# Sliding-window attention: both parts of the keys in one score matmul, summed on VectorE

## The reference

```python
s = jnp.einsum('bcqhgd,bckhd->bchgqk', qc, kb) * (D ** -0.5)
sink = sinks.reshape(1, 1, Hkv, G, 1, 1)
m = jnp.maximum(jnp.max(s, axis=-1, keepdims=True), sink)
e = jnp.exp(s - m)
p = e / (jnp.sum(e, axis=-1, keepdims=True) + jnp.exp(sink - m))
out = jnp.einsum('bchgqk,bckhd->bcqhgd', p, vb)
...
x = x + rmsnorm(out @ w_out, g[1])
h = rmsnorm(x, g[2])
```

## Time and profile before

| what | before |
|---|---|
| runs | 2272.24, 2273.50, 2275.01 us |
| profiled execution: span on the core | 2273.9 us |
| mean granted TensorE clock | 0.993 of full |
| PE busy | 2234.7 us (98%), 11331 matmuls |
| DVE, ACT, POOL busy | 1756.8 (77%), 1183.6 (52%), 840.9 us (37%) |
| steps of the sliding attention (first `turn` to last) | 1452.5 to 1603.4 us |

### The profile page before, as it was taken

How to read it: one execution, slowest core, us unless ns; L and a number is a source line. 1 busy time by engine, 2 the same in 40 slices (tenths; PEclk the granted TensorE clock), 3 DMA queues, 4 the chain that set the end, 5 groups by cost and what they waited for, 6 DMA issues and landing times. The chain is left out here.

```text
span 2273.9 us, 31830 instructions
## 1 busy us (share of the span) xinstructions
PE 2234.7 (98%) x11331; PEld 1890.4 (83%) x11331; DVE 1756.8 (77%) x2694; ACT 1183.6 (52%) x1951; POOL 840.9 (37%) x750
## 2 busy tenths in 40 slices
PE   7999999999999999999999999999999999999998
PEld 6888889999888888888888878888888888888886
DVE  4886789955547888888799867756598888888986
ACT  5658888766433444444444644655444444434453
POOL 3103346310001677777400022222047777771000
PEclk9999999999999999999999999999999999999999
DMA  5111110000422222222663542411322222228435
GB/s 168 36 43 54 29 38 29 11 1 1 167 102 62 77 84 84 84 84 84 217 219 102 185 133 61 107 38 57 108 68 84 84 84 84 84 71 302 150 126 184
DMA packets 190360, 215.18 MB, mean 95 GB/s; under 512 B 15508, under 2 KB 136692, under 8 KB 190204
## 3 DMA queue, kind: packets, MB, share of 16 engines
q1 hardware_dynamic: 185052, 195.81, 27.3%
q10 hardware_dynamic: 5152, 17.34, 2.0%
HBM read 170.77 MB, written 39.98 MB: 93 GB/s over the span
## 5 line engine op out<-in xcount | busy, mean ns | idle before, releaser
L123 PE MATMUL trunk_ps<-l_bhi,l_ahi 128*128 128x512 f32 x528 | 206.0, 390 | 0.5 <-DVE l_blo L3014 0.4
L123 PE MATMUL trunk_ps<-l_bhi,l_alo 128*128 128x512 f32 x528 | 205.5, 389 | 0.0
L123 PE MATMUL trunk_ps<-l_blo,l_ahi 128*128 128x512 f32 x528 | 205.5, 389 | 0.0
L123 PE MATMUL trunk_ps<-l_t_hi,l_s_lo 128*128 128x512 f32 x456 | 177.4, 389 | 0.0
L123 PE MATMUL trunk_ps<-l_t_lo,l_s_hi 128*128 128x512 f32 x456 | 177.4, 389 | 0.0
L123 PE MATMUL trunk_ps<-l_t_hi,l_s_hi 128*128 128x512 f32 x456 | 177.4, 389 | 0.0
L2628 POOL TENSOR_TENSOR l_s_lo<-l_raw,l_s_hi 128x512 fp32r<-128x512 f32 x90 | 157.7, 1760 | 44.9 <-ACT l_s_hi L2539 44.9
L2415 ACT ACTIVATE l_ahi<-l_a 128x512 fp32r<-128x512 f32 x132 | 83.3, 631 | 158.5 <-PE trunk_ps L123 141.5
L2628 POOL TENSOR_TENSOR l_s_lo<-l_w_sum,l_s_hi 128x512 fp32r<-128x512 f32 x76 | 120.0, 1580 | 57.1 <-ACT l_s_hi L2539 56.9
L216 POOL TENSOR_TENSOR wring_w_lo<-wring_raw,wring_w_hi 128x256 fp32r<-128x256 f32 x72 | 56.7, 820 | 192.8 <-ACT wring_w_hi L211 192.8
L123 PE MATMUL trunk_ps<-rest_hi,l_s_lo 128*128 128x512 f32 x304 | 118.3, 389 | 0.0
(11 more groups left out here) (485 smaller groups left out, 6732.7 us busy)
## 6 DMA issues: line engine op xcount, KB each, us to landing
l_draw<-in_ffn_w_out SPq DMA_DIRECT2D x154, 256.0 KB, 2.8
l_raw<-in_ffn_w_in SPq DMA_DIRECT2D x48, 512.0 KB, 4.6
gated_dram<-l_gate_out SPq DMA_DIRECT2D x44, 512.0 KB, 2.6
l_a<-gated_dram SPq DMA_DIRECT2D x88, 256.0 KB, 3.9
wring_raw<-in_even_w_in SPq DMA_DIRECT2D x20, 512.0 KB, 3.9
l_raw_g<-in_ffn_w_in SPq DMA_DIRECT2D x20, 512.0 KB, 3.8
l_raw_v<-in_ffn_w_in SPq DMA_DIRECT2D x20, 512.0 KB, 4.9
l_wt<-in_ffn_w_out SPq DMA_DIRECT2D x22, 256.0 KB, 6.4
```

The costliest lines, as they stand in the source:

```text
L123: mm = pe.matmul(o, w, m, start=a, stop=z, skip_group_check=onto)
```

## The change

The two parts of the keys of one head lie side by side (`keys[kv]`, hi then lo), and a pair's scores are one matmul whose moving operand is 2 x 128 columns (2 x 64 for chunk 0): hi products land in one half of a 256-column output, lo products in the other. The scores of all four pairs now fill the whole of `ps[0]`, so steps n and n+1 share one tile and PE waits for `S_summed` of step n-1 pair by pair. ScalarE copies the lo half of two pairs at a time into `s_lo` (`lo_scores`, L1067 of the new kernel). VectorE's `greatest` is, for each pair, one `tensor_tensor_reduce` (L1377): -0.125 times the sum of the hi half in PSUM and `s_lo`, written to `prob[n % 3]`, with the minimum of these and the negated sink as `nbias`. ScalarE's `exp` works in place on `prob` with scale -1. `prob` has three buffers, the third where the last query group lay. ScalarE's order changes: `lo_scores(n+1)`, `copy(n)`, `exp(n+1)`, `sink_exp(n)`; and ahead of slot 0 as in the diff.

```diff
-        self.prob = [at(f"prob{i}", [P, self.PAIRS, P], F32, W + 2 * KB * i) for i in range(2)]
...
-        self.k_hi = [at(f"k_hi{i}", [P, T], F32R, k_at + 4 * KB * i) for i in range(2)]
-        self.k_lo = [at(f"k_lo{i}", [P, T], F32R, k_at + 4 * KB * (2 + i)) for i in range(2)]
+        self.keys = [at(f"k{i}", [P, 2, T], F32R, k_at + 8 * KB * i) for i in range(2)]
+        self.k_hi, self.k_lo = ([k[:, part, :] for k in self.keys] for part in range(2))
...
+        self.prob = [at(f"prob{i}", [P, self.PAIRS, P], F32, a) for i, a in enumerate((W, W + 2 * KB, fm_at + 8 * KB))]
...
+        self.s_lo = at("s_lo", [P, self.PAIRS, P], F32, K + 128 * KB)
...
-        self.S, self.TR = ([ps[i][:, HALF * h:HALF * h + HALF] for h in range(2)] for i in (0, 1))
+        self.S = ps[0].rearrange("p (u part k) -> p u part k", u=self.PAIRS, part=2)
+        self.TR = [ps[1][:, HALF * h:HALF * h + HALF] for h in range(2)]
...
+        def lo_scores(n):
+            nk = self.keys_of(self.where(n)[1])
+            if n:
+                sc.wait_ge(self.S_summed, 4 * n)
+            for h in range(2):
+                sc.wait_ge(self.S_ready, 2 * n + h + 1)
+                pair = slice(2 * h, 2 * h + 2)
+                sc.activation(self.s_lo[:, pair, 0:nk], self.S[:, pair, 1, 0:nk], ACT.Copy).then_inc(self.S_lo, 1)
+
         def exp(n):
             nk = self.keys_of(self.where(n)[1])
-            sc.wait_ge(self.nb_ready, n + 1)
-            if n >= 2:
-                sc.wait_ge(self.T_ready, n - 1)
             for u in range(self.PAIRS):
-                ins = sc.activation(self.prob[n % 2][:, u, 0:nk], self.S[n % 2][:, u * P:u * P + nk], ACT.Exp,
-                                    bias=self.nbias[:, n % self.ROWS, u:u + 1], scale=0.125)
+                if u % 2 == 0:
+                    sc.wait_ge(self.S_summed, 4 * n + u + 2)
+                prob = self.prob[n % 3][:, u, 0:nk]
+                ins = sc.activation(prob, prob, ACT.Exp, bias=self.nbias[:, n % self.ROWS, u:u + 1], scale=-1.0)
             ins.then_inc(self.exp_done, 1)
...
+        lo_scores(0)
+        pack_queries(N_V - 1)
         exp(0)
-        pack_queries(N_V - 1)
+        lo_scores(1)
+        take(N_V)
         exp(1)
-        take(N_V)
+        lo_scores(2)
         for n in range(self.LAST_SLOT):
+            if 2 <= n < NG - 1:
+                lo_scores(n + 1)
+            if n < NG:
+                copy(n)
             if 1 <= n < NG - 1:
                 exp(n + 1)
             if n < NG:
-                copy(n)
                 sink_exp(n)
...
-            if n >= 2:
-                pe.wait_ge(self.exp_done, n - 1)
             for u in range(self.PAIRS):
-                out = self.S[n % 2][:, u * P:u * P + self.keys_of(c)]
-                queries = self.queries_of(self.PAIRS * kv + u, c)
-                pe.matmul(out, queries, self.k_hi[kv][:, self.window(c)], start=True, stop=False)
-                mm = pe.matmul(out, queries, self.k_lo[kv][:, self.window(c)], start=False, stop=True)
-            mm.then_inc(self.S_ready, 1)
+                if n and u % 2 == 0:
+                    pe.wait_ge(self.S_summed, 4 * (n - 1) + u + 2)
+                mm = pe.matmul(self.S[:, u, :, 0:self.keys_of(c)], self.queries_of(self.PAIRS * kv + u, c), self.keys[kv][:, :, self.window(c)],
+                               start=True, stop=True)
+                if u % 2:
+                    mm.then_inc(self.S_ready, 1)
...
-                mm = pe.transpose(self.TR[n % 2][0:nk, u * P:(u + 1) * P], self.prob[n % 2][:, u, 0:nk], ident)
+                mm = pe.transpose(self.TR[n % 2][0:nk, u * P:(u + 1) * P], self.prob[n % 3][:, u, 0:nk], ident)
...
-            dve.wait_ge(self.S_ready, n + 1)
-            dve.tensor_reduce(self.mx[:, n % self.ROWS, :], self.S[n % 2].rearrange("p (u k) -> p u k", u=self.PAIRS)[:, :, 0:self.keys_of(c)],
-                              AX.X, ALU.max).then_inc(self.mx_ready, 1)
-            dve.wait_ge(self.mx_ready, n + 1)
-            dve.scalar_tensor_tensor(out=self.nbias[:, n % self.ROWS, :], in0=self.mx[:, n % self.ROWS, :], scalar=-0.125,
-                                     in1=self.nsink[:, self.PAIRS * kv:self.PAIRS * kv + self.PAIRS], op0=ALU.mult, op1=ALU.min).then_inc(self.nb_ready, 1)
-            dve.wait_ge(self.nb_ready, n + 1)
+            nk, row, pairs = self.keys_of(c), n % self.ROWS, slice(self.PAIRS * kv, self.PAIRS * kv + self.PAIRS)
+            if n >= 3:
+                dve.wait_ge(self.T_ready, n - 2)
+            if n >= self.ROWS:
+                dve.wait_ge(self.exp_done, n - self.ROWS + 1)
+            for u in range(self.PAIRS):
+                if u % 2 == 0:
+                    dve.wait_ge(self.S_lo, 2 * n + u // 2 + 1)
+                i = self.PAIRS * kv + u
+                dve.tensor_tensor_reduce(self.prob[n % 3][:, u, 0:nk], self.S[:, u, 0, 0:nk], self.s_lo[:, u, 0:nk], -0.125, self.nsink[:, i:i + 1],
+                                         ALU.add, ALU.min, self.nbias[:, row, u:u + 1]).then_inc(self.S_summed, 1)
+            dve.wait_ge(self.S_summed, 4 * n + 4)
             if n >= self.ROWS:
                 dve.wait_ge(self.es_done, n - self.ROWS + 1)
-            dve.tensor_tensor(self.arg[:, n % self.ROWS, :], self.nbias[:, n % self.ROWS, :],
-                              self.nsink[:, self.PAIRS * kv:self.PAIRS * kv + self.PAIRS], ALU.subtract).then_inc(self.arg_ready, 1)
+            dve.tensor_tensor(self.arg[:, row, :], self.nbias[:, row, :], self.nsink[:, pairs], ALU.subtract).then_inc(self.arg_ready, 1)
```

More of the change, by code:

```diff
@@ L909, in __init__ @@
         rows = [self.ROWS, self.PAIRS]
-        self.mx, self.nbias, self.arg, self.es, self.den, self.inv = (
-            at(x, [P] + rows, F32, small + 96 + 128 * i) for i, x in enumerate(("mx", "nbias", "arg", "es", "den", "inv")))
+        self.nbias, self.arg, self.es, self.den, self.inv = (
+            at(x, [P] + rows, F32, small + 96 + 128 * i) for i, x in enumerate(("nbias", "arg", "es", "den", "inv")))
+        self.s_lo = at("s_lo", [P, self.PAIRS, P], F32, K + 128 * KB)
         self.ss, self.var, self.rstd = stats
@@ L927, in __init__ @@
         self.key_hi, self.key_lo, self.q_hi, self.q_lo = (st.sem(x) for x in ("key_hi", "key_lo", "q_hi", "q_lo"))
-        self.S_ready, self.mx_ready, self.nb_ready, self.arg_ready, self.exp_done, self.es_done = (
-            st.sem(x) for x in ("S_ready", "mx_ready", "nb_ready", "arg_ready", "exp_done", "es_done"))
+        self.S_ready, self.S_lo, self.S_summed, self.arg_ready, self.exp_done, self.es_done = (
+            st.sem(x) for x in ("S_ready", "S_lo", "S_summed", "arg_ready", "exp_done", "es_done"))
         self.T_ready, self.copied, self.O_ready, self.den_ready, self.inv_ready, self.O_taken = (
```

## The result

The changed kernel took 2280.11 us (median of 15 runs, 2276.75 to 2281.16), the kernel before 2273.99 (15 runs, 2271.60 to 2277.55). The medians differ by 6.1 us. The ratio is 1.0022, with a 95% interval of 1.0016 to 1.0029: slower by 3.6 to 6.6 us. The forecast was a difference of 3.65 us (0.16%) and a time of 2277.0.

A forecast was written before the change was run, and what follows sets the result against it. PE, busy 98% of the span, was taken to set the pace unless a ScalarE and VectorE chain ran later. 5.75 + 1.35 + 1.05 + 1.2 + 4.75 + 0.3 - 10.75 = +3.65 us gave 2277.0, range 2268 to 2284.

The forecast's parts named there:

- hand-over: Ahead of slot 0: lo parts wait behind table load, exponentials, copies and fused operations; PE restarts at 1455.6, +5.75 us (4.5 to 6.5).
- clock, up to the first turn: After PE's long idle before step 2's scores: half clock slows fifteen transposes, +1.35 us (0 to 5).
- slots 1 to 5: From PE's restart to its first output product: ScalarE's longer work per slot makes 15.1 us into 16.2, +1.05 (0 to 2.5).
- wait for the weights' lo part: Slot 6: `weights_lo(4)` comes behind `greatest(7)`, which waits for lo copies, so the product needing it waits, +1.2 us (0 to 2).
- every fourth slot: Slots 11, 15, 19, 23, 27: PE waits about 0.95 us for the lo part freeing `U`, +4.75 us (0 to 8).
- `take_y` against the next product: Once per row block: its 0.43 us margin before the next block's first product goes; up to 0.1 in six slots, +0.3.
- score matmuls: Slots 6 to 30: four wide matmuls take 0.50 instead of 0.93 us, 25 x 0.43, -10.75 us (10.0 to 11.3 saved).
- (c): Rival, slower: PE stays at the lower clock from restart to the dense slots, some 3.5 us more, 2280.5; chance 0.15.
- (a): Rival: hand-over costs as forecast, but fourth-slot and weight chains find slack, -2.6 us, 2271; chance 0.18.
- (b): Rival, faster: slots 1 to 5 swallow most of the late start and no chain bites, 2265; chance 0.10.
- (d): Rival, slower: ScalarE's queue falls behind in other dense slots, 0.2 us in 23 slots, +4.6, 2281.5; chance 0.10.
- (e): Rival: a matmul's time goes with its columns, so nothing is saved, +14.4 us, 2288; chance 0.03.

The follow-up runs named there:

- the matmuls without use: Changed kernel plus 26 extra 512-column matmuls, results thrown away, in PE's idle time ahead of step 2's scores: 2277.57 us, ratio 1.0014.
- the first edit: Changed kernel with step 0's exponentials and step 1's lo scores put ahead of the last query group's hi parts on ScalarE: 2270.66 us, ratio 0.9985.
- both edits: Changed kernel with the first edit, and VectorE's lo part that frees `U` put ahead of the step's scores in every fourth slot: 2266.36 us, ratio 0.9964.
- the early table: Changed kernel plus a single-column exponential before the last query group's hi parts, so the table loads early: 2277.33 us, ratio 1.0013.
- the version with one wait: Changed kernel with PE waiting once per score set, in front of the first pair, instead of twice: 2279.36 us, ratio 1.0021.
- the narrow version: Changed kernel with each pair's scores again as two matmuls of 128 columns, all else as changed: 2286.64 us, ratio 1.0060.

## Why the prediction came out as it did

The time lay in the range and the mechanisms were mostly those of the walk. The median, 2280.1, lies past the 2278.0 that I had called the border, on the slower side, to which I had given 0.42 against 0.48 for no change. The terms, forecast and found in the stage:

| term | forecast | found |
|---|---|---|
| hand-over | +5.75 | +5.07 |
| clock, up to the first turn | +1.35 | +1.43 (1.87, less 0.44 of step 2's score set) |
| slots 1 to 5 | +1.05 | +1.71 |
| wait for the weights' lo part | +1.2 | 0 |
| second fall of the clock | none | +1.25 |
| every fourth slot | +4.75 | +3.4 |
| `take_y` against the next product | +0.3 | +0.9 |
| score matmuls | -10.75 | -9.5 |
| sum | +3.65 | +4.2 |

That the sum is so near is luck in good part: the terms miss by 7.1 us in all, counted without signs, and by 0.55 with them.

**The hand-over was right, link by link.** The table load behind the last hi parts, then exponentials, copies, four fused operations, lo parts; restart forecast 1455.6, found 1455.37. But the stage began 0.45 later in this trace, so the term is +5.07 and not +5.75. 0.61 of the difference stands ahead of the chain: the last rope began that much earlier in the stage, at 1442.09 and without the wait of 0.97 us for the DMA that swaps halves which it had before (1442.25); why is open. Moving the chain gave back 7.6 us, loading the table early 1.6 (1.3 of it in the chain), and filling the idle time 2.0 by way of the clock. The forecast had named 7.1 for hand-over and clock together.

**The clock's first fall was right, the second was not foreseen.** The fall costs 1.87 us up to the first turn, as the matmuls without use show, 1.46 in the transposes and 0.41 in the score set ahead of them, which the forecast had left out; that set's own saving of 0.44, left out too, brings the net back to 1.43. The premise was weaker than the forecast had it: the gap of 2.29 us of the earlier trace rows stands in every kernel here, and in three of the ten profiled executions (the first edit, both edits, the early table) the clock did not fall near it. In the gap ahead of step 2's scores it fell in each of the four executions where that gap was 6.2 to 6.5 us long and stood empty, and with the early table, where it was 5.2, too. As to the second fall, I had the clock only as a consequence of PE's long wait and as rival (c), one fall that lasts. It recovered in time and fell again in or behind slots 2 to 5, which leave PE partly busy. Eight of the nine executions of the changed kernel and its versions have such a fall, and the one without it has the same program up to there as one with it: the change makes the fall possible, not certain. The earlier trace rows could not show that, and the walk through the slots, which had ScalarE setting their pace, did not ask for it.

**Slots 1 to 5** had their direction and the upper half of their bounds. ScalarE is busy 7.82 of 8 us there, as assumed, and moving two weight blocks out of slots 1 and 2 only moved the wait to the first lo part.

**The wait for `weights_lo(4)` was wrong.** The step that failed is "comes behind `greatest(7)`, I find it 1.2 late": it stood on walked times of slots 4 to 6, and slot 5 ran longer on PE than walked (7.4 us against 6.15 before, by the fall of the clock in it), so the weights came in time, by 0.1 us: they are done at 1484.41, and the product starts at 1484.51. Where no fall lies in slot 5 (both edits, early table), a wait of 0.2 us for `odd_mlo` does appear, and slot 7 takes 5.43 us against 4.94, 0.5 where I had 1.2. That this term and the second fall cancel to 0.05 us is luck.

**The fourth slots were right in kind and mis-sized.** `take_y` starts at 1513.24 and `odd_act_lo` ends at 1528.25 + 0.68 = 1528.93, that is 15.69 us later, forecast 15.7:

```profile
1513.24 1.02 ACT L1109 ACTIVATE main_cos<-trunk_ps 128x1024 f32<-128x1024 f32 x1 [0.31 <-PE trunk_ps L123]
```

```profile
1528.25 0.68 DVE L1406 TENSOR_TENSOR odd_act_lo<-trunk_ps,odd_act_hi 128x512 fp32r<-128x512 f32 x1
```

Each costs 0.84 instead of 0.95, because three score sets save 1.1 us and not 1.3. And there are four, not five: slot 10 has no use of `U`, so nothing in slot 11 waits for the last one. That is a miscount in my list of slots.

**`take_y`** ate its 0.43 us and 0.1 more in slots 13, 17, 21, 25 and 29, as bounded, but 0.4 in slot 9.

**The score matmuls** save 0.38 a slot, not 0.43, and the mis-sized step is "four wide matmuls take 4 x 0.12 + 0.02 = 0.50". The set takes 0.56, of which 0.20 lie between its first and second start and 0.12, as forecast, between any later two and up to the transpose. The waits in the set are not the reason, as the version with one wait shows. Nor is the width: behind an output product the set takes 0.48, four times 0.12, and the narrow set of before is 0.09 shorter there as well (0.84 against 0.93). So 0.08 to 0.09 of a set goes with the transposes ahead of it, in both kernels, and the forecast, which divided 0.93 by eight, put it into the price of each narrow matmul and left it out for the wide ones. The bound of 10.0 was 0.5 too high.

**The rivals.** (a) and (b) fall with the missing slack. (c) came true in a part, as a second short fall. (d) is absent: dense slots show no wait but the four and what `take_y` costs. (e), that time goes with columns, is refuted by the narrow version. By the Trainium skill's isolated gap nothing would have been saved either, and the runs do not agree.

**The base** was misread, by comparing a span with a median of times: the profiled execution stood 1.7 us over the median, not 0.4. That did not move the forecast, which takes the 0.4 off again and so stands on the median (2273.5 + 3.65 = 2277.15; it gives 2277.0); the median of 15 runs came out 0.5 higher. The difference forecast, not its base, carries the comparison: +3.65 against +4.3 between the traces and +6.1 between the medians, with the 1.8 between accounted for above. What made that execution of the kernel before 1.7 us slower than its median is not shown.

## What to carry to other kernels

Where matmuls of 128 and 256 columns follow each other at the same distance in the trace, join two that share the stationary operand, and read the pace of both shapes at like places of the program: what stands ahead of a set is part of its time. Then walk the queues of the helper engines at every hand-over: here an idle stretch that had hidden a table load and a step's exponentials stood right beside the new work, and two reorderings turned +0.22% into -0.36%. Before two executions are compared, hold their granted clocks against each other stretch by stretch: here one that had a fall and one that had not differed by up to 1.25 us in the same stage. Look also at the one operation per round that frees a shared tile, and put it ahead of whatever has got a longer chain.

## What the runs showed of the hardware

Behind four 128-column transposes the first wide matmul starts 0.20 us before the second, where the later ones follow at 0.12, with one wait or two; behind a 512-column product all follow at 0.12. The narrow sets show the same in smaller steps (0.14 us and 0.06 to the second, 0.11 between the later ones), and either way a set behind transposes is 0.08 to 0.09 us longer. What that time is spent on is not shown.

The clock needed no pause to fall: PE was busy 6.24 of the 8 us before the second fall, and no single wait there was over 0.8 us. In the kernel before a stretch of the same stage with PE busy 7.62 of 8 us kept the full clock. With the first edit and with both, the same program with PE busy 6.77 and 6.76 of 8 us was followed by a fall in one execution and by none in the other, so these busy times do not tell which stretch falls:

```profile
1456.00:1464.00 8.00, 7.62 (x63) 6.94 (x61) 6.66 (x17) 6.41 (x19) 2.78 (x4) 1.00 1.03 230
```

A fused sum with minimum of 128 columns with a third operand is 0.27 us from start to start, with 0.08 for the accumulator inside that pitch; the layer 0 rows had 0.28.
